# A recurrent mixer's end: the head norm moved into the scan, outputs turned in quarters, the first group's end beside the second's last round

## The reference, cut to what matters

```
def rwkv7_scan(r, w, k, v, kk, a, S):
    def step(S, inp):
        rt, wt, kt, vt, kkt, at = inp
        sa = jnp.einsum("bhvk,bhk->bhv", S, -kkt)
        S = S * wt[:, :, None, :] + sa[..., None] * (kkt * at)[:, :, None, :] + vt[..., None] * kt[:, :, None, :]
        return S, jnp.einsum("bhvk,bhk->bhv", S, rt)

def head_layernorm(y, w, b, n_heads, out_dtype):          # 16 heads of 64
    mu = jnp.mean(yf, axis=-1, keepdims=True)
    var = jnp.mean(jnp.square(yf - mu), axis=-1, keepdims=True)
    yn = ((yf - mu) * lax.rsqrt(var + RW_LN_EPS)).reshape(bn, L, W)
    return (yn * w + b)

def rwkv_out(y, p, kvec, lnx, w_o):
    y = head_layernorm(from_heads(y), lnx[0], lnx[1], RW_HEADS, r.dtype)
    bonus = jnp.sum((r * k * kvec[2]).reshape(...), axis=-1, keepdims=True) * v.reshape(...)
    return ((y + bonus.reshape(bn, L, D)) * g) @ w_o
```

## Time and profile before

| | before |
|---|---|
| median of 3 runs | 3184.28 us (3184.06 to 3189.78) |
| profiled execution: its own time | 3182.56 us |
| its span | 3180.4 us |
| mean granted TensorE clock | 0.954 |
| busy, share of the span | PE 91%, PEld 76%, DVE 52%, ACT 38%, POOL 4% |
| chain that ended last | PE 78%, DVE 13%, ACT 5% |

### The profile page before, as it was taken

One profiled execution on the slowest core, in us unless ns is written; L12 is line 12 of the kernel. 1 busy time (PEld: TensorE's weight loads), 2 busy tenths in 40 slices (PEclk: granted clock), 3 DMA queues, 4 the chain that ended last, 5 costly groups with the idle time before them and its releaser, 6 DMA issues.

```text
span 3180.4 us, 65560 instructions
## 1 busy us (share of the span) xinstructions
PE 2900.4 (91%) x28304; PEld 2432.8 (76%) x28304; DVE 1658.3 (52%) x2450; ACT 1222.3 (38%) x1849; POOL 117.8 (4%) x152
## 2 busy tenths in 40 slices
PE   6999999999999998998977999886998999996997
PEld 6977799899777987776656777673548988994886
DVE  4546555455565554214556777344324544555885
ACT  4445554444555443223434232232113334331333
POOL 0000000000000000000000000000002222220000
PEclk9999999999999999997888999998999999998999
DMA  5544445455443543441001334221200000002343
GB/s 213 179 165 163 145 149 183 171 180 179 172 169 110 180 169 119 172 146 42 2 23 67 145 147 146 88 75 46 93 27 10 4 4 17 4 4 106 125 154 106
DMA packets 49982, 349.86 MB, mean 110 GB/s; under 512 B 5792, under 2 KB 5792, under 8 KB 9248
## 3 DMA queue, kind: packets, MB, share of 16 engines
q1 hardware_dynamic: 49248, 343.56, 30.4%
q0 software_dynamic: 448, 2.11, 0.2%
HBM read 344.61 MB, written 1.05 MB: 109 GB/s over the span
## 4 chain that ended last, share of the span: by engine, by line
PE 78%; DVE 13%; ACT 5%; issue 2%; DMA 1%; DVEq 0%; SPq 0%; ACTq 0%
PE psum L165 77%; DVE arena L98 3%; DVE wide L87 2%; DVE ring_low L87 2%; DVE arena L87 2%; ACT w_high L144 1%; PE psum L170 1%; DMA ring<-in_evt 1%; ACT arena L140 1%; ACT wide L138 1%; DMA ring<-in_f_gu 1%; DVE x_low L87 0%; ACT L138 0%; DVE wide L98 0%; DVE ntmp L94 0%
## 5 line engine op out<-in xcount | busy, mean ns | idle before, releaser
L87 DVE TENSOR_TENSOR ring_low<-ring,w_high 128x2048 fp32r<-128x2048 f32 (+3 forms) x254 | 560.3, 2206 | 594.2 <-ACT w_high L144 589.5
L144 ACT ACTIVATE w_high<-ring 128x2048 fp32r<-128x2048 f32 (+3 forms) x254 | 468.9, 1846 | 831.0 <-PE psum L165 482.9
L165 PE MATMUL psum<-x_high,w_high 128*128 128x256 f32 (+1 forms) x2040 | 633.4, 310 | 13.0 <-DVE x_low L87 6.7
L165 PE MATMUL psum<-x_high,ring_low 128*128 128x256 f32 (+1 forms) x2040 | 626.6, 307 | 0.0
L165 PE MATMUL psum<-x_low,w_high 128*128 128x256 f32 (+1 forms) x2040 | 626.4, 307 | 0.0
L165 PE MATMUL psum<-wide,ring 64*64 64x64 f32 (+3 forms) x4400 | 410.9, 266 | 30.3 <-issue 16.8
L165 PEld LDWEIGHTS psum<-x_high,w_high 128*128 128x128 f32 x2040 | 390.0, 191 | 49.6 <-issue 16.8
L165 PEld LDWEIGHTS psum<-x_high,ring_low 128*128 128x128 f32 x2040 | 389.9, 191 | 18.6
L165 PEld LDWEIGHTS psum<-x_low,w_high 128*128 128x128 f32 x2040 | 390.3, 191 | 17.1
L165 PEld LDWEIGHTS psum<-wide,ring 64*64 64x64 f32 (+2 forms) x4400 | 292.6, 145 | 126.9 <-issue 97.1
L165 PE MATMUL psum<-w_high,x_high 128*128 128x512 f32 (+2 forms) x720 | 281.3, 391 | 15.6 <-issue 13.7
(11 more groups left out here) (191 smaller groups left out, 3447.4 us busy)
## 6 DMA issues: line engine op xcount, KB each, us to landing
ring<-in_f_gu SPq DMA_DIRECT2D x88, 1024.0 KB, 4.8
ring<-in_w_mod SPq DMA_DIRECT2D x48, 1024.0 KB, 5.0
ring<-in_fu SPq DMA_DIRECT2D x44, 1024.0 KB, 4.8
ring<-in_f_dn SPq DMA_DIRECT2D x40, 1024.0 KB, 4.8
ring<-in_w_in SPq DMA_DIRECT2D x28, 1024.0 KB, 4.8
ring<-in_fd SPq DMA_DIRECT2D x20, 1024.0 KB, 4.9
ring<-in_rkvr SPq DMA_DIRECT2D x12, 1024.0 KB, 4.8
ring<-in_w_out SPq DMA_DIRECT2D x8, 1024.0 KB, 4.9
```

Source lines behind the costliest of these rows:

```text
L87: self.done(self.eng.tensor_tensor(o, a, b, op), then)
L144: self.done(self.eng.activation(o, i, ACT.Copy, scale=scale), then)
L165: ins = self.eng.matmul(o, l, r, start=a, stop=z)
```

## The change

Four things are changed.

The norm's statistics are taken chunk by chunk: when a group's backward chunk 12, 13, 14 or 15 has been added to its output, VectorE takes sum, difference, square and sum of squares for these 128x256, in the step after `y`. Round 16 ends with the scaling and the reciprocal for the group's 16 columns, ScalarE's root, and four products that scale the chunks. ScalarE loads the root's table in round 16 of group 0.

The outputs are turned in quarters (`turned_pe`): eight 64x64 products with `eye`, one for each chunk and half, so that both halves arrive in a bank at once as 128x256. VectorE then needs two instructions for a pair: a scalar_tensor_tensor (scale, add the bonus) and the product by the gate. The bias of `lnx` is added to the bonus beforehand, in rounds 1 to 8. The result lies in `KK`, not `XT`.

This end is part of each group's generator (`outputs_pe`, `outputs_act`, `outputs_dve`), so group 0's four pairs are written among the second group's last round.

The output product waits for each pair's `yg_ok` instead of the last one, and the three `AFTER_SCAN` loads wait for the scan's last `y` product of each group.

```diff
@@ -2371,9 +2371,10 @@
...
         sc_p = [signal(f"sc_p{g}", [(n, x) for n in range(16) for x in ("br", "mj1", "mj2", "mj3")]) for g in TWO]
-        on_ok, onr_ok, onn_ok = [signal(n, [0]) for n in ("on_ok", "onr_ok", "onn_ok")]
+        on_ok, onr_ok, onn_ok = [signal(n, TWO) for n in ("on_ok", "onr_ok", "onn_ok")]
         yt2_mm, rg_mm, yg_ok = [signal(n, range(8)) for n in ("yt2_mm", "rg_mm", "yg_ok")]
         yc_ok = signal("yc_ok", range(8))
+        NM, NV, NR = [x.rearrange("p (c k) -> p c k", c=4) for x in (small[:, 0:32], small[:, 32:64], small[:, 112:144])]
         wo_mm = signal("wo_mm", TWO)
...
@@ -2486,6 +2487,10 @@
...
                 yield
+                if n == 16:
+                    yield
+                    yield
+                    return
                 if new:
...
@@ -2529,6 +2534,44 @@
...
 
+        def turned_pe(T, k):
+            g = k // 4
+            w = raw(("rg2",))
+            b = 4 * g + k % 2
+            T.bank(b, yc_ok[k])
+            T.eng.wait_ge(*onn_ok[g])
+            for c in FOUR:
+                for i in TWO:
+                    p = slice(64 * i, 64 * i + 64)
+                    T.mm(bank(b)[p, 64 * c:64 * c + 64], YZ[p, c, k, :], eye[p, :], True, True,
+                         yt2_mm(k) if c == 3 and i else None)
+            T.eng.wait_ge(*landed(("rg2",)))
+            T.bank(b + 2, yg_ok[k])
+            T.mm(bank(b + 2)[:, 0:256], w[:, 128 * k:128 * k + 128], GS, True, True,
+                 w_free(("rg2",)) if k == 7 else rg_mm(k))
+
+        def outputs_pe(T, g):
+            yield from scan_pe(T, g)
+            for k in range(4 * g, 4 * g + 4):
+                turned_pe(T, k)
+                yield
+
+        def outputs_act(A, g):
+            yield from scan_act(A, g)
+            for _ in FOUR:
+                yield
+
+        def outputs_dve(D, g):
+            yield from scan_dve(D, g)
+            for k in range(4 * g, 4 * g + 4):
+                y = KK[:, k, 0:256]
+                D.eng.wait_ge(*yt2_mm[k])
+                D.stt(y, bank(4 * g + k % 2)[:, 0:256], lx[:, 0, k:k + 1], BV[:, k, :], ALU.mult, ALU.add, yc_ok(k))
+                D.eng.wait_ge(*(w_free[("rg2",)] if k == 7 else rg_mm[k]))
+                D.tt(y, y, bank(4 * g + 2 + k % 2)[:, 0:256], ALU.mult, yg_ok(k))
+                yield
+
         def scan_act(A, g):
...
@@ -2566,7 +2609,15 @@
...
                     A.copy(lt, double(g, (n, "lta"))[:, 0], a_((n, "lta")))
-                yield
+                if n == 16 and g == 0:
+                    A.act(small[:, 216:217], ident[:, 0:1], ACT.Sqrt)
+                yield
+                if n == 16:
+                    yield
+                    se.wait_ge(*on_ok[g])
+                    A.act(NR[:, :, 4 * g:4 * g + 4], NR[:, :, 4 * g:4 * g + 4], ACT.Sqrt, onr_ok(g))
+                    yield
+                    return
                 if new:
...
@@ -2671,6 +2722,25 @@
...
                 yield
+                if m >= 12:
+                    c = chunk(m) - 4
+                    y, s, a = YZ[:, c, hs, :], ntmp[:, :].rearrange("p (k v) -> p k v", k=4), NM[:, c, hs]
+                    D.red(a, y, ALU.add)
+                    D.stt(y, bc(a, 64), -1.0 / 64, y, ALU.mult, ALU.add)
+                    D.tt(s, y, y, ALU.mult)
+                    D.red(NV[:, c, hs], s, ALU.add)
+                elif old and m < 8 and g == 0:
+                    D.tsc(BV[:, m, :], BV[:, m, :], lx[:, 1, m:m + 1], None, ALU.add, None)
+                if n == 16:
+                    D.tsc(NV[:, :, hs], NV[:, :, hs], 1.0 / 64, 64e-5, ALU.mult, ALU.add)
+                    D.recip(NR[:, :, hs], NV[:, :, hs], on_ok(g))
+                    yield
+                    ve.wait_ge(*onr_ok[g])
+                    for c in FOUR:
+                        y = YZ[:, c, hs, :]
+                        D.tt(y, y, bc(NR[:, c, hs], 64), ALU.mult, onn_ok(g) if c == 3 else None)
+                    yield
+                    return
                 yield
...
@@ -2787,18 +2857,8 @@
...
             te.wait_ge(*vz_a[7])
-            lead(scan_pe(T, 0), scan_pe(T, 1))
-            te.wait_ge(*onn_ok[0])
-            te.wait_ge(*landed(("rg2",)))
-            w = raw(("rg2",))
-            for k in range(8):
-                T.bank(k % 4, yc_ok[k])
-                trs(T, [(bank(k % 4)[0:64, 128 * c:128 * c + 128], YZ[:, c, k, :]) for c in FOUR], yt2_mm(k))
-                T.bank(4 + k % 4, yg_ok[k])
-                T.mm(bank(4 + k % 4)[:, 0:256], w[:, 128 * k:128 * k + 128], GS, True, True,
-                     w_free(("rg2",)) if k == 7 else rg_mm(k))
+            lead(outputs_pe(T, 0), outputs_pe(T, 1))
             gate_pe(T, ("r", 0))
-            te.wait_ge(*yg_ok[7])
             for n in TWO:
...
@@ -2809,10 +2869,12 @@
...
                         for k in FOUR:
+                            if n == 0 and tb == 0:
+                                te.wait_ge(*yg_ok[4 * g + k])
                             then = None
...
                                 then = w_free(key) if tb else wo_mm(n) if g else None
-                            T.mm(bank(b), XT[:, 4 * g + k, 128 * tb:128 * tb + 128], w[:, 512 * k:512 * k + 512],
+                            T.mm(bank(b), KK[:, 4 * g + k, 128 * tb:128 * tb + 128], w[:, 512 * k:512 * k + 512],
                                  g == 0 and k == 0, g == 1 and k == 3, then)
...
@@ -2857,9 +2919,7 @@
...
                 value_rows(A, i, 0, vz_a(i))
-            lead(scan_act(A, 0), scan_act(A, 1))
-            se.wait_ge(*on_ok[0])
-            A.act(small[:, 112:144], small[:, 112:144], ACT.Sqrt, onr_ok(0))
+            lead(outputs_act(A, 0), outputs_act(A, 1))
             se.wait_ge(*yg_ok[7])
...
@@ -2967,30 +3027,7 @@
...
                 D.tt(BV[:, i, :], bank(2 + i % 2)[:, 0:256], VT[:, i, 256:512], ALU.mult, rw_dve(("bv", i)))
-            lead(scan_dve(D, 0), scan_dve(D, 1))
-            Y3 = YZ.rearrange("p c k v -> p (c k) v")
-            S3 = wide[:, 0:2048].rearrange("p (n v) -> p n v", v=64)
-            a_, b_, c_ = small[:, 0:32], small[:, 32:64], small[:, 112:144]
-            D.red(a_, Y3, ALU.add)
-            D.tsc(a_, a_, 1.0 / 64, None, ALU.mult, None)
-            D.tt(Y3, Y3, bc(a_, 64), ALU.subtract)
-            D.tt(S3, Y3, Y3, ALU.mult)
-            D.red(a_, S3, ALU.add)
-            D.tsc(b_, a_, 1.0 / 64, 64e-5, ALU.mult, ALU.add)
-            D.recip(c_, b_, on_ok(0))
-            ve.wait_ge(*onr_ok[0])
-            D.tt(Y3, Y3, bc(c_, 64), ALU.mult, onn_ok(0))
-            for k in range(8):
-                ve.wait_ge(*yt2_mm[k])
-                p4 = bank(k % 4)[0:64, :].rearrange("p (c h t) -> p c h t", c=4, h=2)
-                y = XT[:, k, 0:256]
-                for a in TWO:
-                    D.copy(y[64 * a:64 * a + 64, :].rearrange("p (c t) -> p c t", c=4), p4[:, :, a, :],
-                           yc_ok(k) if a else None)
-                D.tsc(y, y, lx[:, 0, k:k + 1], lx[:, 1, k:k + 1], ALU.mult, ALU.add)
-                D.tt(y, y, BV[:, k, :], ALU.add)
-                ve.wait_ge(*(w_free[("rg2",)] if k == 7 else rg_mm[k]))
-                D.tt(y, y, bank(4 + k % 4)[:, 0:256], ALU.mult, yg_ok(k))
+            lead(outputs_dve(D, 0), outputs_dve(D, 1))
             split_three(split_dve, D, 4)
...
@@ -3083,7 +3120,8 @@
...
                 if key in AFTER_SCAN:
-                    eng.wait_ge(*on_ok[0])
+                    for g in TWO:
+                        eng.wait_ge(*sc_mm[g][15, "y"])
                 eng.dma_start(raw(key), src).then_inc(slot_in[slot_of[key]], 16)
...
```

## The result

The changed kernel took 3174.53 us (median of 6 runs, 3171.94 to 3175.80), the kernel before 3188.70 (6 runs, the three known at first and three beside the changed one, 3184.06 to 3192.33): a ratio of 0.9955, 95% interval 0.9945 to 0.9966, or 14.2 us less. 3167.5 was forecast, with a range of 3163 to 3174: the direction was right, the time came out half a microsecond above the range. The forecast of -16.5 us is a ratio of 0.9948. By the interval the gain is 10.8 to 17.5 us, so the whole runs alone don't tell 14.2 from the 16.5 that was forecast; the traces show where the difference arises.

The account below looks back on a forecast made before the run. TensorE bounds the kernel, with a 33.05 us hole behind the scan where it follows VectorE. Terms: -15.3 (earlier output product), -1.65 (its full clock), +0.5 (scan) = -16.5 us; forecast 3167.5 us, range 3163 to 3174.

Parts of the forecast that it names:

- k4 to the output product: Second group's four features, two at half clock, plus about 1.0 us of gate broadcasts; output product at 2892.7.
- the blocks hide in the two holes: Scan rounds 13 to 15: VectorE's 1.92 us blocks fit its 2.39 and 1.66 us waits, costing 0.5 us in all.
- the new wait of TensorE for the scaled chunks: Before the second group's `q4`: the first turned feature waits for all four scaled chunks until 2872.15, some 2 us.
- So `y` starts at 2872.15 + 4 x 1.08 + 1.9 = 2878.4: Second group's last round: four features of 1.08 us and 1.9 us of products precede `y`, making it 5.5 us later.
- The seams: TensorE's changes between 64x64 tiles and the whole array: 0.09 us each, two per feature; bounds 0 and 0.28.
- (b): After the scan: dearer seams and half clock cost some 6 us more, 3173; chance 0.17 together with (e).
- (a): In the scan: half of the blocks' 11.5 us shows, 5.75 instead of 0.5, giving 3173; chance 0.14.
- (c): Tail: seams and clock cost nothing, 1.4 + 1.6 us more gained, giving 3164.5; chance 0.65 together with the forecast.
- (d): Scan: 15.2 us of VectorE insertions delay both groups' chains, up to 30 us lost, 3198; slower; chance 0.04.
- (e): Second group's last round: first group's end pushes it back by its whole length, 3173; chance 0.17 together with (b).
- a scan that ends over 8 us late: Sign in the changed trace: a scan ending more than 8 us late makes the forecast wrong.
- an output product after 2897: Sign in the changed trace: an output product starting after 2897, where 2892.7 was forecast, makes the forecast wrong.

Follow-up runs that it names:

- e4_rwo: Changed kernel with the output product's first quarter placed before the second group's features, in TensorE's hole; stretch -22.1 us, ratio 0.9938 to the kernel before.
- e8b_busy: Changed kernel with 160 unused TensorE records in its wait for the second group's norm; stretch -15.0 us, ratio 0.9954 to the kernel before.
- e2_apart: Changed kernel with all eight features behind both scans, the norm still chunk by chunk; stretch -16.8 us, ratio 0.9939 to the kernel before.
- e7b_pairs: Changed kernel with two turnings and then two gate broadcasts on TensorE, halving tile changes; stretch -15.6 us, ratio 0.9954 to the kernel before.
- e1_turn: Kernel before with only the new turning and outputs, head norm in one piece behind the scan; stretch -8.9 us, ratio 0.9976 to the kernel before.
- e5_both: e4_rwo with the first group's features behind both scans; stretch -21.7 us, ratio 0.9932 to the kernel before.
- e10_order: e4_rwo with k0 ahead of the second group's `us`, k1 ahead of its `y`, k2 and k3 behind; stretch -22.6 us, ratio 0.9925 to before.
- e11_order_pairs: e10_order with k2 and k3, k4 and k5, k6 and k7 issued in pairs; stretch -22.8 us, ratio 0.9927 to the kernel before.
- e6b_more: Changed kernel with square and sum of squares done three times in rounds 13 to 15; stretch -4.8 us, ratio 0.9985 to the kernel before.

## Why the prediction was right, and where it failed

The forecast's clock readings are in the time of before. Those of after are put beside them less 6.25 us: 5.83 from ahead of the scan, and 0.42 by which the scan was longer.

| step | forecast | measured |
|---|---|---|
| the scan up to g0's last `y` | +0.5 | +0.42 |
| g1's `q3` sum late by | 1.15 (its terms add up to 1.09) | 0.93 |
| first turned feature (waits for the scalings) | 2872.15 | 2872.18 |
| from it to g1's last `y` sum | 7.9 | 10.0 |
| g1's last `y` sum starts | 2880.06 | 2882.18 |
| from that to k4 | 5.0 | 4.98 |
| k4 to the output product | 7.6 | 8.34 |
| the output product starts | 2892.7 | 2895.50 |
| the output product lasts | 27.7 | 27.63 |
| change over the stretch | -16.5 | -13.8 |

The forecast of 3167.5 was 7.0 us low. Two terms make 7.2 of it: 2.8 in the change, all in the turned features, and 4.4 in the base.

**Right.** The mechanism, step by step: the blocks hide in the two holes; the new wait of TensorE for the scaled chunks, in front of `q4`, came within 0.03 us of its place and at 2.12 us; g1's chunk, reciprocal, root and scalings took what was forecast; the broadcasts lie in front of the output product; that runs at full clock. The table load, now at 2869.24 beside products, cost nothing. The weights were no limit either: the last three loads were issued at 2888.50, and none of the four took over 9.0 us.

**Wrong: "So `y` starts at 2872.15 + 4 x 1.08 + 1.9 = 2878.4".** The four features in front of g1's `y` were mis-sized, by 2.1 us. The sizes of both parts are shown. A feature takes 1.24 us at full clock, not 1.08 (e4_rwo, e8b_busy): the changes of tile cost 0.14 and 0.20, not 0.09 each. Four times 0.16 is 0.6. And a half-clock stretch of 3.4 us fell into them, which the forecast had only behind them: 1.5 us (8.34 against e4_rwo's 6.83). It fell in three of the four executions in which TensorE has these instructions; why it fell stays open. Without it the change would have come out at -15.3 in this trace, so half of the miss hangs on the execution.

**Wrong, the same term again: k4 to the output product, 7.6.** Measured 8.34, of it 1.7 for the clock (6.65 in e8b_busy), which was forecast at 1.6. The seams are the remaining 0.6. The two together are the 2.8 us by which the change fell short. The trace of before showed one seam with 64x64 tiles only, towards 64x128; of the two ends that I had, 0 and 0.28, the truth lay near the middle and I chose a third. The earlier trace rows even holds a change that costs nothing that can be seen: the old turning goes between 128x64 tiles and the whole array, and its four and two records follow each other by 0.44 and 0.43 us, which is what such records take without a change (in the changed kernel's trace the 16 broadcasts of 128x128 take 1.78 from start to start, so 0.44 for four; the 64 records of 512 columns take 27.63, so 0.43 for two of half the width). The Trainium skill ("TensorEngine Tiling (Array Packing)", Key Properties) says that a change of the tiling mode drains the engine. By that rule, with the 0.28 of the earlier trace rows at every seam, the sixteen seams would have been charged 3.0 us over the forecast; 1.3 was measured. So the traces show a cost at each change between 64x64 and the whole array, but not the full 0.28, and none between 128x64 and the whole array.

**Rivals.** (b), the dearer end, is what happened, with less than half of its price, and its clock part elsewhere: not in the gate's broadcasts and the output product, which ran at full clock, but in front of `y`. Its seams came on both sides. Its own terms add up to 6.6 us and 3174.1, not to "some 6, 3173": the range ended just below it. (a) did not happen, but little was left: in the changed kernel VectorE's idle time in front of g1's `q3` sum is down from 2.39 to 0.56 us, and in front of its `n3` sum there is none. (c) is excluded: seams and clock do cost. (d) would have needed over 1 us lost for each inserted; the scan lost 0.4 at most for the blocks' 11. (e), the first group's end pushing back the second's, is what e2_apart shows: g1's last `y` sum came 7.6 us later than before instead of 5.5. By the sign that was set for it, a scan that ends over 8 us late, the forecast stood on the edge (8.06 from the scan's start); by the other, an output product after 2897, it held (2895.50). What I failed to weigh is e2_apart: placing g0's features in front of g1's `q4` buys nothing if TensorE then has a hole of 5 us anyway, behind g1's `y`. That part of the change lost some 3 us.

**The base.** The change was set against 3184.28, the median of three runs. Later sets of the same kernel gave medians of 3187.50 (15 runs), 3189.62 (15), 3190.56 (11) and 3188.49 (9). 3167.5 + 2.8 + 4.4 (3188.70 - 3184.28) = 3174.7. The profiled execution had the same bias: 3182.56, with the scan starting earlier than in any other trace. Between 1471 and 1497 us its mean clock was 0.87, the changed kernel's 0.74: 0.13 x 26 is 3.4 us by this estimate, and the ScalarE copies near both ends put the loss at 3.1 of the 5.83. The other 2.7 arise in smaller pieces up to the scan. What makes the clock drop there in one execution and not in another is open; no run here was made on it.

## What to carry to other kernels

Work that is moved ahead of a wait is paid in full if the wait's end hangs on the same engine: move into a hole only what the hole's end doesn't need (here a quarter of the next product, 6.9 us of TensorE's work), and leave in front of the last critical product nothing that can stand behind it. When an engine waits and the trace names no releaser, look at who last reads the buffer that it will write. And a forecast time rests on its base as much as on the change: here the change was 2.8 us off and the base 4.4. A single profiled execution carries its own half-clock stretches, here up to 2.5 us in one place: compare two kernels' traces piece by piece, with the clock beside them, before a difference of that size is put down to an edit.

## What the runs showed that was not expected

- A change from 64x64 tiles to the whole array costs TensorE 0.14 us and the way back 0.20 (e4_rwo, e7b_pairs). The one seam from 64x64 to 64x128 in the trace of before was 0.09, and between 128x64 and the whole array there was none to be seen.
- TensorE's clock stood at half after holes of 3.19 us (e2_apart), 5.03 (the changed kernel) and 13.22 (e1_turn), and was not lowered after those of 1.10 (e5_both), 1.15 (e10_order) and 1.49 (e11_order_pairs). Around the wait of 2.1 us in front of `q4` four executions in which TensorE has the same instructions differ: it fell within the wait in e8b_busy, within the first feature behind it in e6b_more, 1.8 us behind its end in the changed kernel, and not at all in e4_rwo.
- The scalar_tensor_tensor with a constant factor and a broadcast column of `small` took 0.42 us; the one with a factor from `prm` 0.48, as in the earlier trace rows. Started while a GpSimd product ran, the first took 0.61. In the same place the product of two SBUF operands, which took 0.84 beside GpSimd in the earlier trace rows, had none beside it and took 0.43. Who starts first counts: in the scan of before, the VectorE products of two SBUF operands that started while a GpSimd product ran took 0.83 or 0.84, and those that started 0.04 to 0.20 us ahead of one took 0.42 or 0.43.
